# A two-block transformer kernel in float32: p's weights split in eight pieces among the out-projection's tiles, and one gate tile's split held back

## The reference

```python
h = (o * jax.nn.silu(z)) @ w_out                                # out-projection, 1024 -> 1024
x = layer_norm(DEEPNORM_ALPHA * x + h, ln_g[i], ln_b[i])        # mean, variance over the features
gate = jax.nn.sigmoid(x @ ple_w_gate[i])                        # gate, 1024 -> 1024
x = x + gate * (p[i] @ ple_w_proj[i])                           # p has 256 features
```

## Time and profile before

| | |
|---|---|
| median of 3 runs | 2666.68 us (2660.0 to 2669.28) |
| the profiled execution | 2666.65 us, its span 2664.4 us |
| PE busy | 2543.3 us, 95% of the span |
| POOL busy | 1579.1 us, 59% |
| DVE busy | 1401.5 us, 53% |
| ACT busy | 751.6 us, 28% |

### The profile page before, as it was taken

The page is one execution under the profiler, slowest core; times in us unless marked ns, Lnnn a source line. Parts: engine busy times, 40 slices in busy tenths (PEclk is TensorE's granted clock), DMA queues, the critical chain, the costliest instruction groups (busy, mean ns, idle before and its releaser), DMA issues.

```text
span 2664.4 us, 39702 instructions
## 1 busy us (share of the span) xinstructions
PE 2543.3 (95%) x14594; PEld 2097.1 (79%) x14594; DVE 1401.5 (53%) x2058; ACT 751.6 (28%) x1566; POOL 1579.1 (59%) x1669
## 2 busy tenths in 40 slices
PE   5999989999999999999999999999999999999999
PEld 4878978888888886888788887778788887677776
DVE  4863556753663758725433333454454454637754
ACT  3224353111111123245321212222222223314423
POOL 2533324765675664442777777776666664664464
PEclk9999999999999999999999999999999999999999
DMA  6341142332332322111223332433333332232221
GB/s 247 117 153 40 40 158 88 119 126 63 126 126 79 121 77 67 56 59 39 88 93 95 95 95 87 135 103 101 93 93 103 101 95 74 72 102 72 80 95 63
DMA packets 79262, 255.55 MB, mean 96 GB/s; under 512 B 9872, under 2 KB 13712, under 8 KB 78864
## 3 DMA queue, kind: packets, MB, share of 16 engines
q1 hardware_dynamic: 61280, 210.59, 24.4%
q10 hardware_dynamic: 17840, 43.03, 5.3%
HBM read 236.28 MB, written 2.10 MB: 89 GB/s over the span
## 4 chain that ended last, share of the span: by engine, by line
PE 42%; POOL 30%; issue 19%; DVE 4%; ACT 1%; DMA 1%; POOLq 1%; SPq 1%; DVEq 0%; ACTq 0%
POOL w_lo L428 17%; POOL w_hi L426 10%; PE PS L434 8%; PE PS L437 8%; PE PS L435 8%; PE PS L1511 4%; PE PS L1512 4%; PE PS L1513 4%; POOL word L421 2%; PE PS L1384 1%; DVE XL L2240 1%; DMA modt<-in_wmod 1%; PE PS L1700 1%; DVE X L1166 1%; DVE Z L2233 1%
## 5 line engine op out<-in xcount | busy, mean ns | idle before, releaser
L428 POOL TENSOR_TENSOR w_lo<-raw,w_hi 128x512 fp32r<-128x512 f32 (+1 forms) x662 | 957.4, 1446 | 55.3
L434 PE MATMUL PS<-XH,w_hi 128*128 128x512 f32 x2168 | 821.1, 379 | 33.5 <-DVE XL L2600 8.2
L435 PE MATMUL PS<-XL,w_hi 128*128 128x512 f32 x2168 | 792.9, 374 | 0.0
L437 PE MATMUL PS<-XH,w_lo 128*128 128x512 f32 x2168 | 743.6, 374 | 0.0
L421 POOL TENSOR_TENSOR word<-ones 128x1 f32<-128x1 f32 x331 | 99.2, 300 | 1015.8 <-PE PS L437 675.8
L426 POOL TENSOR_SCALAR w_hi<-raw 128x512 fp32r<-128x512 f32 (+1 forms) x662 | 531.9, 803 | 0.0
L434 PEld LDWEIGHTS PS<-XH,w_hi 128*128 128x128 f32 x2168 | 410.6, 189 | 140.6 <-issue 15.3
L435 PEld LDWEIGHTS PS<-XL,w_hi 128*128 128x128 f32 x2168 | 410.8, 189 | 73.9
L437 PEld LDWEIGHTS PS<-XH,w_lo 128*128 128x128 f32 x2168 | 380.5, 189 | 59.4
L1511 PE MATMUL PS<-XH,w_hi 128*128 128x512 f32 (+1 forms) x640 | 231.9, 362 | 8.2 <-DVE XL L2240 8.2
L1512 PE MATMUL PS<-XL,w_hi 128*128 128x512 f32 (+1 forms) x640 | 226.5, 354 | 0.0
(11 more groups left out here) (332 smaller groups left out, 3215.4 us busy)
## 6 DMA issues: line engine op xcount, KB each, us to landing
raw<-in_wgu SPq DMA_DIRECT2D x88, 512.0 KB, 3.5
raw<-in_wa SPq DMA_DIRECT2D x80, 512.0 KB, 3.5
modt<-in_wmod SPq DMA_DIRECT2D x48, 512.0 KB, 10.1
raw<-in_win SPq DMA_DIRECT2D x48, 512.0 KB, 3.6
modv<-in_wmod ACTq DMA_DIRECT2D x48, 512.0 KB, 4.9
raw<-in_wdn SPq DMA_DIRECT2D x32, 512.0 KB, 3.6
QS<-Z ACTq DMA_DIRECT2D x100, 128.0 KB, 2.9
raw<-in_wout SPq DMA_DIRECT2D x16, 512.0 KB, 3.4
```

The lines of the kernel that those rows point to most:

```text
L428: pool.tensor_tensor(lo, src, hi.bitcast(FP32), ALU.subtract).then_inc(s_split, 1)
L434: pe.matmul(acc(s)[:, a:b], hi, rh[:, i, a:b], start=i == 0, stop=False)
L435: pe.matmul(acc(s)[:, a:b], hi, rl[:, i, a:b], start=False, stop=False)
L437: last = pe.matmul(acc(s)[:, a:b], lo, rh[:, i, a:b], start=False, stop=i == k - 1)
```

## The change

On POOL, p's weights are no longer split in one go between the last out tile and the first gate tile. They are split in eight pieces, one for each p tile (2 of 16 chunks, 128x256): none behind out tiles 0 to 2, piece 0 behind tile 3, pieces 1 and 2 behind tile 4, 3 and 4 behind 5, 5 and 6 behind 6, piece 7 behind tile 7. Each piece is a tensor_scalar to PWH and a tensor_tensor to PWL. The loops of two rounds are written out. The split of the second gate tile (u == 1) waits until DVE has made all eight subtractions of the mean (s_lnd). On PE, each p tile waits for its own piece.

```diff
         def second_pool(pool):
-            def eight(s):
-                with pool.Fori(0, 2) as i:
-                    for u in range(4):
-                        split_weights(pool, s + u, 4 * i)
-
-            def ple(l):
-                pool.wait_ge(s_pw, 16 * (l + 1))
-                pool.tensor_scalar(PWH[:], PWR[:], 1.0, 0.0, ALU.mult, ALU.add).then_inc(s_pwh, 1)
-                pool.wait_ge(s_pwh, l + 1)
-                pool.tensor_tensor(PWL[:], PWR[:], PWH[:].bitcast(FP32), ALU.subtract).then_inc(s_pwl, 1)
-                eight(N_PLE[l])
+            def p_weights(l, u):
+                at = slice(2 * u, 2 * u + 2)
+                if u == 0:
+                    pool.wait_ge(s_pw, 16 * (l + 1))
+                pool.tensor_scalar(PWH[:, at], PWR[:, at], 1.0, 0.0, ALU.mult, ALU.add).then_inc(s_pwh, 1)
+                pool.wait_ge(s_pwh, KT * l + u + 1)
+                pool.tensor_tensor(PWL[:, at], PWR[:, at], PWH[:, at].bitcast(FP32), ALU.subtract).then_inc(s_pwl, 1)
+
+            def out_and_ple(l, s):
+                for u in range(KT):
+                    split_weights(pool, s + u)
+                    for piece in ((), (), (), (0,), (1, 2), (3, 4), (5, 6), (7,))[u]:
+                        p_weights(l, piece)
+                for u in range(KT):
+                    if u == 1:
+                        pool.wait_ge(s_lnd, KT * (l + 1))
+                    split_weights(pool, N_PLE[l] + u)
...
-            eight(N_AOUT)
-            ple(0)
+            out_and_ple(0, N_AOUT)
...
-            eight(N_BOUT)
-            ple(1)
+            out_and_ple(1, N_BOUT)
...
                 if u == 0:
                     pe.wait_ge(s_pl, l + 1)
-                    pe.wait_ge(s_pwl, l + 1)
+                pe.wait_ge(s_pwl, KT * l + u + 1)
```

## The result

| | before | after |
|---|---|---|
| median of the runs | 2662.07 us (2657.19 to 2669.28, 20 runs) | 2667.82 us (2662.49 to 2677.72, 20 runs) |
| ratio, 95% interval | 1 | 1.0024 [1.0015, 1.0033] |
| the profiled execution, span | 2666.65, 2664.4 | 2672.18, 2670.4 |

The change costs 6.4 us (4.0 to 8.8 by the interval): slower, and less than the 0.3% (8.0 us) that the prediction takes as what a measurement tells from no change. Forecast were +5.3 us on the profiled execution, 2672.0.

A forecast was written before the change was run, and what follows sets the result against it. Bound: a PE matmul stream (42% of the chain) fed by POOL's weight splitting (30%). Layer 0 +4.0 - 1.9 = +2.1, layer 1 +5.1 - 1.9 = +3.2, together +5.3 on 2666.65: 2672.0 us, range 2662 to 2678.

The forecast's parts named there:

- a, a piece: POOL: one 256-column piece takes 0.39 and 0.69, with the gap 1.15 us; bounds 0.86 and 1.96.
- b, the load: POOL: PWR's load lands before tile 3's split ends at 2272.87, so no wait from there.
- c, POOL's queue: POOL from 2272.87, layer 0: splits, seven pieces and turns with VectorE take 29.15 us; tile 7's split ends about 2302.0.
- d, PE's waits: PE, layer 0: waits about 1.0, 2.1 and 1.7 us before tiles 5 to 7; tile 7 ends 2305.3 instead of 2300.58.
- e and f, the mean's sum: Start of the sum for the mean behind the out tiles: 4.0 us later in layer 0, 5.1 later in layer 1.
- g, the hold: Second gate split waits for VectorE's subtractions: gain 1.9 us per layer, bounds 0 and 2.85; 3.1 us of cover.
- h, the rest: Last piece, first gate split, p tiles' own waits (bound 3 us) and written-out loops (0.65 per layer either way): taken 0.
- The clock: PE's granted clock after the waits before the late out tiles: no fall, taken 0, with 3.4 us kept as a bound.
- rival 3: POOL bounds and more goes wrong: clock falls in tile 6 or 7 (+3.4) or dearer pieces (+5.6); 2675 to 2678, chance 0.18.
- (1): POOL between tiles 3 and 7: pieces disappear in its spare time, -6.1 us, 2660.5; chance 0.12.
- (2): Pieces near 0.86 us or fewer turns lost with VectorE: 2 us less per layer, 2668 or a little under; chance 0.18.
- (4): First gate split lasts into the subtractions, so the hold does not act: +3.8 us, 2675.8; chance 0.04.

The follow-up runs named there:

- four pieces ahead: The changed kernel, hold included, with four pieces ahead of the end of tile 7's split instead of seven; ratio to before 0.9999 [0.9989, 1.0010].
- three, two and three: The changed kernel with pieces 0 to 2 behind tile 7, 3 and 4 between hold and second gate split, 5 to 7 behind it; ratio to before 1.0004.

## Why the prediction came out

Each step against its rows, layer 0 first:

- **a, a piece.** 1.15 forecast, 0.41 + 0.74 measured, 1.18 from start to start: the straight line through two sizes held at a size that no row had shown.
- **b, the load.** POOL waits for PWR nowhere in the stage.
- **c, POOL's queue.** Tile 7's split was to end 28.85 us behind tile 2's copy; it ended 28.93 behind. POOL never stood still: 31.58 of 33 us.
- **d, PE's waits.** Forecast 1.0, 2.1 and 1.7; idle was 0.94, 1.39 and 1.35, and counted by the copies the tiles came 1.23, 1.73 and 1.66 later than 5.49 apart. Tile 7 is late by 4.63 where 4.7 (2305.3 less 2300.58) was forecast. The total held in part by luck, as two misses cancel: its first half came 26.20 behind tile 2's copy (forecast 26.65), but a tile behind a wait takes 5.82 to 5.86 us from its first matmul to its copy, where 5.5 was taken. The middle wait was put too high. The wait for PWL went, as said.
- **e and f, the mean's sum.** +4.0 and +5.1 forecast, +3.92 and +5.33 measured. Tile 7's addition to TH did release it ([0.37 <-DVE TH] above). The reason given for the difference of the layers is wrong, though, as told below the list.
- **g, the hold.** 1.9 per layer forecast, 2.07 and 2.06 measured, with the first square 0.38 sooner and the squares in 7.13 (forecast 0.4 and 7.4). The cover of the held split was 3.35 us (ready at 2324.81, needed at 2328.16), forecast 3.1. The size is right but the step gives all of it to the hold. Without the hold the changed kernel's step is 0.97 longer; the other 1.10 came from the later mean, as moving the mean moved the subtractions off the second gate split. The step fixed POOL where it was and did not ask where that split would lie without the hold. With the kernel before's order, where the mean isn't late, the hold alone gives 1.7.
- **h, the rest.** The first gate split ended at 2313.36, ahead of the mean; the p tiles waited nowhere for their pieces. The written-out loops and the p tiles' own waits cost nothing to be seen: with all eight pieces behind tile 7, where both are present, tile 7 is on pace (27.47).
- **The clock.** Taken as 0, and the time bore that out. But the reason given holds for layer 0 only: waits of 0.94 to 1.39 left the granted clock at 1.00. Behind the 2.68 in layer 1 it was 0.74 and 0.78, so the lower level does come between two dense tiles, and rival 3's mechanism did appear. Tile 5 took 7.17 us there from its first matmul (2579.36) to its copy, 5.82 in layer 0. That cost tile 6 at most 0.3 us and tile 7 nothing: tile 5 ended at 2586.53, when ScalarE copied it, and tile 6's first half was split at 2586.20; tile 6 ended at 2592.07 and tile 7's first half was split at 2593.37. PE only waited less for POOL. The Trainium skill ("TensorE: Matmul & The Clock Gate", Part 1) says that the lower rate is the default and returns after an idle stretch; this case's row of 2.68 agrees and its rows of 0.94 to 1.39 show no fall.

**Why the layers differ.** Step f reads POOL's missing wait in layer 1 as no time to spare. But POOL needs 4.84 us for a tile there too (2574.75 to 2579.59, 2579.59 to 2584.43) against PE's 5.49. The layers differ in how long PE's first tiles last at the low clock, and so in how far POOL gets ahead. From ScalarE's copy of tile 0 to that of tile 2 it took 9.93 us in layer 0 and 8.32 in layer 1; POOL then stood idle for 1.39 us ahead of tile 7's split in layer 0, and not at all in layer 1. In the second profile of the kernel before it is the other way round: 8.31 and 10.47 us, idle 0 and 1.93. In the changed kernel POOL alone sets the pace, so there the start no longer counts:

| us from tile 0's copy to tile 7's copy | layer 0 | layer 1 |
|---|---|---|
| before, its two profiles | 37.39, 35.78 | 35.80, 37.94 |
| after, its two profiles | 42.22, 42.32 | 42.21, 42.25 |
| four pieces ahead | 38.83 | 38.89 |

So it is luck that +4.0 and +5.1 came out layer by layer: the changed kernel's execution happened to start as that of the kernel before did, long in layer 0 (10.13) and short in layer 1 (8.37).

**The rivals.** That the pieces disappear in POOL's spare time (1) falls: three waits in layer 0, 4.6 us late. About even (2) falls by its condition, since a piece took 1.18 and not 0.86, and by the interval, +1.3 against a lower end of +4.0. Of rival 3 the clock appeared without its price, and the pieces' price of the 512-column pair did not; the lower end of its range, +8.4, is still inside the timing's interval, so it is the rows that rule it out. That the hold does not act (4) falls for this change, since the first gate split was done before the mean; the runs with the pieces behind tile 7 and with four ahead show what it costs where it isn't. The sum, +5.3, stands against +5.1 by stages and +6.4 [4.0, 8.8] by the runs.

## What to carry to other kernels

A side job cut in pieces hides only in what time the engine has between its due jobs: here POOL could spare some 0.6 us per tile in either layer, and of the seven pieces' 8.3 us ahead of the last tile 4.6 and 6.4 came out as lateness. What hid of them was the lead that POOL had on PE. Part of that lead came while PE's first tiles ran at the low clock, and this part changed from one execution to the next: a wait that is missing in one profile doesn't say that the engine has nothing to spare. Work moved behind that point isn't free either, since it pushes the next job into another engine's stretch; every order tried paid either ahead of the mean, in the subtractions or in the normalisations. The mark up to which a stage is measured has to lie behind all that the moved work can touch: three orders here looked better at the first gate matmul than one tile later. Where a change joins a part that gains with one that loses, as the hold and the pieces here, each is worth running alone: the hold by itself gained 3.7 us by the rows, the whole change lost 5.1.

## What was not expected

**The stretch between the two stages has two rhythms, by chance.** From layer 0's first gate matmul to the start of layer 1's end took 231.99 us before and 227.82 after, with the same code. The spacing of most heads in the attention of layer 1 (YH<-ZS on ScalarE) is 17.31 us in one rhythm and 16.45 in the other. Both kernels show both, each in one of its two profiled executions, so the edit doesn't set the rhythm. The first profile of the kernel before, by line (mean in ns after the busy time), with VectorE's and POOL's timelines:

```profile
L1075 DVE TENSOR_TENSOR QB<-Z,QS 128x512 f32<-128x512 f32 x8 | 8.5, 1058 | 0.3
```

```profile
2454.95 1.13 DVE L1075 TENSOR_TENSOR QB<-Z,QS 128x512 f32<-128x512 f32 x1
```

```profile
2454.93 0.61 POOL L426 TENSOR_SCALAR w_hi<-raw 128x512 fp32r<-128x512 f32 x1
```

And the same kernel again:

```profile
L1075 DVE TENSOR_TENSOR QB<-Z,QS 128x512 f32<-128x512 f32 x8 | 5.9, 732 | 0.3
```

```profile
2455.28 0.69 DVE L1075 TENSOR_TENSOR QB<-Z,QS 128x512 f32<-128x512 f32 x1
```

```profile
2456.41 0.19 POOL L421 TENSOR_TENSOR word<-ones 128x1 f32<-128x1 f32 x1 [3.21 <-PE PS L437]
```

```profile
2469.18 1.10 DVE L1109 TENSOR_TENSOR YL<-ZS,YH 128x512 fp32r<-128x512 f32 x1 [0.72 <-ACT YH L907]
```

In the slow rhythm POOL's w_hi starts 0.02 us ahead of VectorE's addition, which then takes 1.13 instead of 0.69, in the last six of the eight heads; in the fast one POOL comes 1.1 us later. From the first head to the last it takes some 118 us (118 to 120) or some 112: the long way in the first profile of before, the second of after, with the hold alone, with four ahead and with three, two and three; some 112 in the others. That this addition keeps the rhythm isn't shown, and the last line speaks against it as the whole cause: in the fast rhythm it is VectorE's YL that takes 1.10 instead of 0.69 in four heads, and 0.44 us is half of the 0.86 between the spacings. The Trainium skill ("SBUF — State Buffer", "SBUF: two separate sides") says that a VectorE operation with two SBUF inputs and a GpSimd one that reads SBUF lock each other out, the later one waiting; the rows agree, 0.44 us for the addition.

The rhythm isn't all. From the first gate matmul to the first head it took 112.3 and 110.3 us in the kernel before, 114.1 and 114.7 in the changed one, and in the second profile of the changed kernel one of the last heads came 1.6 us late as well; that is how the stretch came to 224.1 and 236.3. With the hold alone, which keeps most of the loops, it took 113.5, and 113.8 with the pieces alone, with four ahead and with all behind tile 7. So a microsecond or two here may come from the edits after all, and no run tells.

A swing of 6 us is as large as the change, and it is why a single pair of profiled executions (2672.18 less 2666.65) agrees with the forecast in part by luck: this stretch was 4.2 us shorter after, and the stage of layer 0 began 5.6 us later in code that the change doesn't touch. A change of this size is read from its stages, and timed over many runs.
